# Attentions and moves stand further up in the order, and ScalarE's queue issues the reads of turned blocks

## The chip, the core and the metric

The kernel runs on one core of a Trainium2 chip. Its engines are TensorE (PE, matrix products into PSUM), VectorE (DVE), ScalarE (ACT), GpSimd (POOL) and SyncE (SP), each with an instruction stream of its own that is worked off strictly in order; they wait for each other by semaphores. Sixteen DMA engines move data between HBM and the on-chip SBUF; a DMA is issued by an instruction in some engine's stream. The metric is the device time of one execution, in microseconds (us).

## What is computed

Two transformer blocks of two layers each, on 256 tokens of width 1024, all in float32. A layer of the first block (only the shapes matter here):

```python
h = x @ w_in[l]                                   # 1024 x 9216: q, k, v of three attentions, and gates
o_a = retention(rq, rk, rv, rg)                   # 4 heads, rotary q and k
o_b = chunk_attention(cq, ck, cv, rel_bias)       # 8 heads
o_c = diff_attention(dq, dk, dv)                  # 8 half heads, rotary q and k
merged = g0 * (o_a @ w_branch_a) + g1 * (o_b @ w_branch_b) + g2 * (o_c @ w_branch_c)
x = layer_norm(ALPHA * x + merged @ w_out)
x = layer_norm(ALPHA * x + swiglu(x))
```

A layer of the second block has a swiglu, a mixer (an mLSTM with a short convolution beside a windowed attention aq, ak, av), a second swiglu and a gated embedding.

## The kernel before

**Dense work.** Every product with a weight is cut into "units": 128x1024 floats of weights (two k-tiles of 512 columns), with 12 matmuls for both row tiles, because each product is made from a high and a low part (weights high x input high, low x high, high x low). There are some 780 units. For unit `u` SP loads `raw` (13 buffers, `NR`), ScalarE makes the high part `wh` (10 buffers, `NH`), VectorE the low part `wl`. SP issues the load of unit u+13 and ScalarE the high part of unit u+10 when unit u is done. A chunk of 512 output columns is four units; it is gathered in one of two pairs of PSUM banks, in turn, and its evacuation (`keep`, `gate`, `merge`) has to be over before the next chunk but one starts in the same banks. `keep` is done by ScalarE.

**Side work.** `plan_block1` and `plan_block2` write the steps down once, as one list, and every engine goes through this list and emits its own part of each step. `weave` puts the attention steps (the side) among the dense units; how many units follow each side step is the digit in a table, `UNITS_AMONG_1` for the first block and `UNITS_AMONG_2` for the second. A digit moved is thus a move on all engines at once.

**Moves.** Where rows have to become columns (the rotated rq, rk, dq, dk, the attention outputs rg0, rg1, oc, and ak, aq0, aq1), VectorE transposes 32x32 blocks (`block`), the blocks are written to a scratch in HBM by four DMAs (`out`), read back in turned order by one (`back`), and ScalarE copies (`copy`) or splits (`halve`, with VectorE for the low part) what has landed. The swiglus do the same for every 256 columns (`act_out`, `act_back`, `split_act`), 11 times in each of the six. Before the change SP issues all of these, between the weight loads.

**The stretch of the first block that matters.** In unit order: dq is projected by units 36 to 39, dk by 40 to 43, dv by 44 to 47 (`keep` after each), the gates of branch a by 48 to 55, and `w_branch_a` with the retention's output `oa` is 56 to 63. Unit 48 uses the banks of dk, unit 52 those of dv, and unit 56 waits for `halve` of rg1. POOL rotates dq and dk (`rope`, 12 operations each, in order, semaphore `roped`). The step `load name="bm12"` has SP load the gates' bias into `b_merge`, memory that it shares with the decay and rotation tables; so SP first waits for the last score product of the retention and for the rotation of dk (lines 1217 to 1219); `ln1` right behind it waits for the rotation too.

In the second block `p_split`, `a_square` and `m_log` are small steps of ScalarE ahead of the first convolution chunk (`conv`), whose evacuation by VectorE frees the banks of `mv0`.

Of the kernel before, what the change touches and what calls it, by code (L numbers as in the profile page):

```python
# [15 lines left out]
P = 128  # L16
# [3 lines left out]
KT = D // P  # L20
# [9 lines left out]
NH = 10  # L30


OUT_AT, BACK_AT, LAST_AT = 0, 2, 4


# [2 lines left out]

UNITS_AMONG_1 = "0101110101110001100001010111322201001101000110011010101213311002101010201102232"
UNITS_AMONG_2 = "10000020101100011211002110001101011110011110401001111100100111101101000101020040102"

# [316 lines left out]
def plan_block1(p, t_x):  # L362
# [109 lines left out]
    for j in range(2):  # L472
        merge(1, j, "w_branch_b", "ob", 4, j, ob_o + 1)
    p.weave(before, dense_a + p.begin(), side, UNITS_AMONG_1)

# [157 lines left out]
def plan_block2(p, t_x):  # L633
# [20 lines left out]

    t_x = ffn("ffn1", 0, t_x, after_ffn1)

    def kept_rows(name, c0, dst, off, pair):
        c = p.chunk(("w_in", [(c0, c0 + 512)]), "x", KT, 512, pair, t_x)
        q[name] = p.add("keep_kv" if name == "akv" else "keep", c=c, dst=dst, off=off)

    def convolved(i, pair):
# [6 lines left out]
    for i, (name, c0, dst, off) in enumerate([("akv", 5128, "aqk", 1024), ("aq0", 4104, "aqk", 0),  # L668
                                              ("aq1", 4616, "aqk", 512)]):
        kept_rows(name, c0, dst, off, (i + 1) % 2)  # L670
        if name == "akv":
            p.add("a_ksquare", kept=q["akv"])
        else:
            if name == "aq0":
                p.add("a_knorm")
                p.moved("block", "ak")
            p.moved("block", name, kept=q[name])
    group = p.begin()
    p.steps = before
    p.open(group, OPEN["w_in_2"])  # L680
    p.pair = 0
    c_log = p.chunk(("w_in", [(4096, 4104)]), "x", KT, 8, p.pair, t_x, form="narrow")
    p.add("m_narrow", c=c_log)
    p.add("p_split")
    for r in range(R):
        p.add("a_square", tile=r, kept=(q["aq0"], q["aq1"]), n=p.cc["sumsq"])
# [6 lines left out]
    for i in range(4):  # L693
# [6 lines left out]
        else:  # L700
            c = p.chunk(("w_in", [(3072 + 512 * (i - 2), 3584 + 512 * (i - 2))]), "x", KT, 512, p.flip(), t_x)
# [12 lines left out]
    p.add("m_log", t=p.next_t(), c=c_log)  # L714
    for r in range(R):
        p.add("a_sum", tile=r)
    for what in ("out", "back", "copy"):
        for name in ("ak", "aq0", "aq1"):
            c_a = p.moved(what, name)
    p.add("m_log2")  # L720
    p.add("m_spread", n=p.of_block["aq1"])
    tt, sm = {}, {}
# [24 lines left out]
    c_a = []  # L747
# [8 lines left out]
    for j in range(2):  # L756
        c = p.chunk(("w_branch_m", [(512 * j, 512 * j + 512)]), "hm", KT, 512, p.flip(), t_m)
# [10 lines left out]
    for j in range(2):  # L768
        c = p.chunk(("w_out", [(512 * j, 512 * j + 512)]), "x", KT, 512, p.flip(), t_g)
# [7 lines left out]
    t_x = p.tail(group, lambda tile: rms(p, 2, tile, fed), turned(p, 2, fed), *TAILS["w_out_2"])  # L777
# [15 lines left out]
    for j in range(2):  # L793
# [5 lines left out]
        c = Step("chunk", u=u, pair=1, nth=nth)  # L799
# [13 lines left out]
        else:  # L813
            t_x = p.tail(group, lambda tile: rms(p, 0, tile, fed), turned(p, 0, fed), *TAILS["ple"])
# [95 lines left out]
MOVED = ('rg0', 'rg1', 'oc', 'rq', 'rk', 'dq', 'dk', 'ak', 'aq0', 'aq1')  # L910
# [4 lines left out]
def build(nc, plan, a):  # L915

    with ExitStack() as ctx:
# [71 lines left out]
        act_out = [sem(f"act_out{i}") for i in range(2)]  # L989
        act_back = [sem(f"act_back{i}") for i in range(2)]  # L990
        act_split = sem("act_split")
        blocked = sem("blocked")
        moved_out = {name: sem("out_" + name) for name in MOVED}
        moved_back = {name: sem("back_" + name) for name in MOVED}
# [12 lines left out]
        x, o = mem.at("x", o, [P, R, D])  # L1007
# [6 lines left out]
        b = {}  # L1014
# [27 lines left out]
        c0 = o  # L1042
# [74 lines left out]
        def of2(w, h):  # L1117
# [13 lines left out]
        landed = {**stage,  # L1131
                  "rg0": b["rg"][:, 0, :],
                  "rg1": b["rg"][:, 1, :]}
# [18 lines left out]
        with nc.Block() as block:  # L1152
            @block.sync
            def _(sp):
# [8 lines left out]
                for st in steps:  # L1163
# [13 lines left out]
                    elif st.kind == "out":  # L1177
                        sp.wait_ge(blocked, st.n)
                        to = a["moved"][MOVED.index(st.name)].rearrange("(q j b n) -> b j q n", q=4, j=32, b=4)
                        for k in range(4):  # L1180
                            sp.dma_start(to[k], stage[st.name][32 * k:32 * k + 32, :].rearrange("p (q n) -> p q n", q=4))\  # L1181
                              .then_inc(moved_out[st.name], 16)
                    elif st.kind == "back":
                        sp.wait_ge(moved_out[st.name], 64 * (st.l + 1))
                        sp.dma_start(landed[st.name], a["moved"][MOVED.index(st.name)].rearrange("(p n) -> p n", p=P))\
                          .then_inc(moved_back[st.name], 16)
                    elif st.kind == "act_out":
                        sp.wait_ge(act_turned, st.n)
                        to = a["turn"][st.i].rearrange("(q j b n) -> b j q n", q=4, j=32, b=4)
                        for k in range(4):  # L1190
                            sp.dma_start(to[k], b["ffn_s"][32 * k:32 * k + 32, st.i % 2, :, :].rearrange("p r n -> p (r n)")
                                         .rearrange("p (q n) -> p q n", q=4)).then_inc(act_out[st.n % 2], 16)
                    elif st.kind == "act_back":
                        sp.wait_ge(act_out[st.n % 2], 64 * ((st.n + 1) // 2))
                        sp.dma_start(b["ffn_a"][:, st.i % 2, :, :].rearrange("p r n -> p (r n)"),
                                     a["turn"][st.i].rearrange("(p n) -> p n", p=P))\
                          .then_inc(act_back[st.n % 2], 16)
                    elif st.kind == "load":
                        k, l = st.name, st.l
                        if k == "bias":  # L1200
# [147 lines left out]
            def _(act):  # L1348
# [7 lines left out]
                for st in steps:  # L1356
                    k = st.kind
# [19 lines left out]
                    elif k == "o_split":  # L1377
                        act.wait_ge(o_ready_0, st.m)
                        act.wait_ge(o_ready, st.o + 1)
                        act.activation(split_of[st.dst][0][:, st.h // 2 - 1:st.h // 2 + 1, :],  # L1380
                                       OB[:, :].rearrange("p (k n) -> p k n", k=2), ACT.Copy).then_inc(t_hi, 1)
                    elif k == "copy":
                        act.wait_ge(moved_back[st.name], 16 * (st.l + 1))
                        act.activation(copy_to[st.name].rearrange("p k (r b n) -> p (k r) b n", r=R, b=4),
# [63 lines left out]
                    elif k == "square":  # L1448
                        r, j = st.tile, st.j
# [20 lines left out]
                    elif k == "conv":  # L1470
                        act.wait_ge(unit_done, st.c.u + 1)
                        act.wait_ge(p_conv, 16 * (st.l + 1))
                        for ct in range(2):
                            c = 2 * st.i + ct
# [19 lines left out]
                    elif k == "a_square":  # L1494
                        r = st.tile
# [860 lines left out]
```

## Time and profile before

| what | value |
| --- | --- |
| median of 3 runs | 2307.84 us (2306.3 to 2308.96) |
| the profiled execution: its own time | 2307.95 us |
| its span in the trace | 2306.2 us |
| TensorE busy | 99% |
| VectorE busy | 66% |
| ScalarE busy | 53% |
| POOL busy | 6% |
| DMA, mean over the span | 209 GB/s |

Busy is time in which an engine executes something; PE's matmuls are pipelined, so 99% busy says that little time lies idle between them, not that each is as short as it can be. An idle time has a releaser: the instruction whose semaphore ended the wait.

### The profile page before, as it was taken

Reading aid. Unit: us, or ns where it says so; the run is one execution under the profiler, and the core shown is the slowest. Engines: PE = TensorE matmul, PEld = TensorE weight load, DVE = VectorE, ACT = ScalarE, POOL = GpSimd, SP = SyncE. Lnnn points to the kernel's source line nnn. Section 1 sums busy time; section 2 is a strip of 40 time slices with the busy share of each in tenths; the row PEclk is TensorE's granted clock in tenths of the full one; section 3 lists DMA queues with packets and bytes.
Section 4 is the critical chain, followed back from the end, with each engine's and each line's share of the span. In section 5 each row is a group of like instructions: output and inputs, shape, how many; then the busy total and the mean of one; then the engine's idle time right before and its main releaser. Section 6 shows DMA issues by size and latency. Waiting matters only on the chain.

```text
span 2306.2 us, 30120 instructions
## 1 busy us (share of the span) xinstructions
PE 2283.7 (99%) x11144; PEld 1906.6 (83%) x11144; DVE 1527.7 (66%) x2411; ACT 1233.8 (53%) x1890; POOL 128.6 (6%) x141
## 2 busy tenths in 40 slices
PE   9999999999999999999999999999999999999999
PEld 8887888888878888888878888888888888888887
DVE  6656786566567866576587765664766587657654
ACT  6555544445555454354467654554554478555543
POOL 3140000004300000000000000000000000000000
PEclk9999999999999999999999999999999999999999
DMA  8556568756475587577564444875677564456772
GB/s 336 199 192 238 190 220 290 228 185 214 156 267 186 172 287 242 180 256 248 189 230 157 157 155 165 265 241 195 219 244 238 178 215 156 150 171 209 233 235 89
DMA packets 179857, 483.08 MB, mean 209 GB/s; under 512 B 20480, under 2 KB 65152, under 8 KB 178688
## 3 DMA queue, kind: packets, MB, share of 16 engines
q1 hardware_dynamic: 179712, 481.16, 61.7%
q8 instruction: 90, 1.47, 0.3%
q14 instruction: 55, 0.45, 0.1%
HBM read 452.24 MB, written 28.84 MB: 209 GB/s over the span
## 4 chain that ended last, share of the span: by engine, by line
PE 92%; DVE 3%; DMA 3%; ACT 1%; SPq 1%; issue 1%; POOL 0%; DVEq 0%; ACTq 0%
PE bank L2104 27%; PE bank L2109 27%; PE bank L2108 27%; PE bank L2151 2%; PE bank L2091 2%; PE bank L2092 2%; PE bank L2093 2%; DMA raw<-in_weights 1%; DVE wl L1593 1%; PE bank L2240 1%; SPq L1181 1%; DMA rg<-moved 1%; DMA moved<-rv 0%; PE bank L2202 0%; PE bank L2225 0%
## 5 line engine op out<-in xcount | busy, mean ns | idle before, releaser
L1363 ACT ACTIVATE wh<-raw 128x1024 fp32r<-128x1024 f32 (+1 forms) x778 | 814.5, 1051 | 768.1 <-PE bank L2109 690.8
L1593 DVE TENSOR_TENSOR wl<-raw,wh 128x1024 fp32r<-128x1024 f32 (+1 forms) x778 | 927.8, 1223 | 282.9 <-ACT wh L1363 279.3
L2104 PE MATMUL bank<-wh,xh 128*128 128x512 f32 (+1 forms) x2102 | 826.8, 393 | 5.0 <-issue 3.9
L2109 PE MATMUL bank<-wh,xl 128*128 128x512 f32 (+1 forms) x2102 | 816.8, 389 | 0.0
L2108 PE MATMUL bank<-wl,xh 128*128 128x512 f32 (+1 forms) x2102 | 815.7, 388 | 0.0
L2104 PEld LDWEIGHTS bank<-wh,xh 128*128 128x128 f32 x2102 | 395.2, 188 | 87.0 <-issue 7.3
L2109 PEld LDWEIGHTS bank<-wh,xl 128*128 128x128 f32 x2102 | 394.9, 188 | 81.0
L2108 PEld LDWEIGHTS bank<-wl,xh 128*128 128x128 f32 x2102 | 395.5, 188 | 76.9
L2104 PE MATMUL bank<-wh,act_h 128*128 128x512 f32 x528 | 206.0, 390 | 0.0
L2109 PE MATMUL bank<-wh,act_l 128*128 128x512 f32 x512 | 199.4, 389 | 0.0
L2108 PE MATMUL bank<-wl,act_h 128*128 128x512 f32 x512 | 199.3, 389 | 0.0
L2104 PEld LDWEIGHTS bank<-wh,act_h 128*128 128x128 f32 x528 | 99.1, 188 | 20.2
L2109 PEld LDWEIGHTS bank<-wh,act_l 128*128 128x128 f32 x512 | 96.1, 188 | 20.0
L2108 PEld LDWEIGHTS bank<-wl,act_h 128*128 128x128 f32 x512 | 96.1, 188 | 19.7
L2091 PE MATMUL bank<-xh,wh 128*128 128x256 f32 x384 | 110.6, 288 | 0.0
L2093 PE MATMUL bank<-xh,wl 128*128 128x256 f32 x384 | 108.6, 283 | 0.0
L2092 PE MATMUL bank<-xl,wh 128*128 128x256 f32 x384 | 108.6, 283 | 0.0
L2030 DVE SCALAR_TENSOR_TENSOR ffn_a<-bank,scr,ffn_s 128x256 f32<-128x256 f32 (+1 forms) x96 | 39.6, 457 | 71.1 <-ACT ffn_s L1559 71.0
L1396 ACT ACTIVATE act_h<-ffn_a 128x512 fp32r<-128x512 f32 x66 | 41.6, 630 | 73.4 <-DMA ffn_a<-turn 73.3
L2091 PEld LDWEIGHTS bank<-xh,wh 128*128 128x128 f32 x384 | 73.5, 191 | 1.4 <-issue 1.0
L2092 PEld LDWEIGHTS bank<-xl,wh 128*128 128x128 f32 x384 | 73.6, 192 | 0.1
L2093 PEld LDWEIGHTS bank<-xh,wl 128*128 128x128 f32 x384 | 73.5, 192 | 0.0
(347 smaller groups left out, 2066.9 us busy)
## 6 DMA issues: line engine op xcount, KB each, us to landing
raw<-in_weights SPq DMA_DIRECT2D x760, 512.0 KB, 4.3
turn<-ffn_s SPq DMA_DIRECT2D x264, 64.0 KB, 2.8
ffn_a<-turn SPq DMA_DIRECT2D x66, 256.0 KB, 4.7
raw<-in_weights SPq DMA_DIRECT2D x16, 384.0 KB, 3.2
ln<-in_ln SPq DMA_DIRECT2D x4, 1024.0 KB, 6.8
moved<-merged SPq DMA_DIRECT2D x32, 128.0 KB, 3.5
merged<-moved SPq DMA_DIRECT2D x8, 512.0 KB, 7.0
bias<-in_bias SPq DMA_DIRECT2D x2, 1024.0 KB, 9.3
```

The source lines that it names most:

```text
L1181: sp.dma_start(to[k], stage[st.name][32 * k:32 * k + 32, :].rearrange("p (q n) -> p q n", q=4))\
L1363: act.activation(wh[:, u % NH, 0:used(u)], raw[:, u % NR, 0:used(u)], ACT.Copy).then_inc(hi_done, 1)
L1396: act.activation(b["act_h"][:, 2 * st.i:2 * st.i + 2, :].rearrange("p k (r b n) -> p (k r) b n", r=R, b=4), act_in(st.i), ACT.Copy).then_i ...
L1593: dve.tensor_tensor(wl[:, u % NR, 0:used(u)], raw[:, u % NR, 0:used(u)], wh[:, u % NH, 0:used(u)].bitcast(F32), ALU.subtract).then_inc(lo_ ...
L2030: ins = dve.scalar_tensor_tensor(dst, up, root[:, r:r + 1], s_in, ALU.mult, ALU.mult)
L2091: pe.matmul(out, w_h, lh[:, kt, :], start=st.first and i == 0, stop=False)
L2092: pe.matmul(out, w_h, ll[:, kt, :], start=False, stop=False)
L2093: last = pe.matmul(out, w_l, lh[:, kt, :], start=False, stop=st.last and i == st.nk - 1)
L2104: pe.matmul(out, h, w_h, start=st.first and i == 0, stop=False)
L2108: pe.matmul(out, h, w_l, start=False, stop=False)
L2109: last = pe.matmul(out, lo, w_h, start=False, stop=ends)
L2151: last = pe.transpose(bank[:, i * P:(i + 1) * P], piece, ident[:, :])
```

## The change

`UNITS_AMONG_1` and `UNITS_AMONG_2` get other digits (the line of one stands here for both); out and back of ak, aq0 and aq1 leave the woven side list and are written among the first chunks of the mixer; and all `back` and `act_back` steps are emitted by ScalarE in place of SP, with the same waits. No computation is added or left out.

```diff
+OUT_EARLY = {1: "ak", 2: "aq0"}
...
-UNITS_AMONG_1 = "0101110101110001100001010111322201001101000110011010101213311002101010201102232"
+UNITS_AMONG_1 = "0101110101110001100001010111012101001101000111011011101213311002101010201102244"
...
+    def out_early(i):
+        if i in OUT_EARLY:
+            p.moved("out", OUT_EARLY[i])
+
     def kept_rows(name, c0, dst, off, pair):
-        c = p.chunk(("w_in", [(c0, c0 + 512)]), "x", KT, 512, pair, t_x)
+        c = p.chunk(("w_in", [(c0, c0 + 512)]), "x", KT, 512, pair, t_x, among=out_early if name == "aq1" else None)
...
+    p.moved("back", "ak")
     group = p.begin()
...
     p.add("m_narrow", c=c_log)
+    p.moved("back", "aq0")
+    p.moved("out", "aq1")
     p.add("p_split")
...
-    for what in ("out", "back", "copy"):
-        for name in ("ak", "aq0", "aq1"):
-            c_a = p.moved(what, name)
+    for name in ("ak", "aq0", "aq1"):
+        if name == "aq1":
+            p.moved("back", name)
+        c_a = p.moved("copy", name)
...
-                    elif st.kind == "back":
-                        sp.wait_ge(moved_out[st.name], 64 * (st.l + 1))
-                        sp.dma_start(landed[st.name], a["moved"][MOVED.index(st.name)].rearrange("(p n) -> p n", p=P))\
-                          .then_inc(moved_back[st.name], 16)
...
-                    elif st.kind == "act_back":
-                        sp.wait_ge(act_out[st.n % 2], 64 * ((st.n + 1) // 2))
...
+                    elif k == "act_back":
+                        act.wait_ge(act_out[st.n % 2], 64 * ((st.n + 1) // 2))
...
+                    elif k == "back":
+                        act.wait_ge(moved_out[st.name], 64 * (st.l + 1))
+                        act.dma_start(landed[st.name], a["moved"][MOVED.index(st.name)].rearrange("(p n) -> p n", p=P))\
+                           .then_inc(moved_back[st.name], 16)
```

**SP in the first block.** These are SP's DMAs of the kernel before, from the read-back of rk to the read-back of rg0. The 24 weight loads are those issued when units 24 to 47 are done; `b_merge` is the load "bm12", `ln` is "ln1", and `rv` is the stage from which rg0 and rg1 go out.

```order
L1185 DMA dv<-moved 128x1024 [waits out_rk]
L1168 DMA raw<-in_weights 128x1024 [waits unit_done] x24
L1219 DMA b_merge<-in_b_merge 128x2048 [waits roped,s_done]
L1222 DMA ln<-in_ln 128x2048 [waits roped]
L1168 DMA raw<-in_weights 128x1024 [waits unit_done]
L1181 DMA moved<-rv 32x4x256 [waits blocked]
L1181 DMA moved<-rv 32x4x256 x3
L1168 DMA raw<-in_weights 128x1024 [waits unit_done]
L1181 DMA moved<-rv 32x4x256 [waits blocked]
L1181 DMA moved<-rv 32x4x256 x3
L1168 DMA raw<-in_weights 128x1024 [waits unit_done]
L1185 DMA rg<-moved 128x1024 [waits out_rg0]
```

And this is the same place in the changed kernel, from the way out of rk on.

```order
L1190 DMA moved<-dv 32x4x256 x3
L1177 DMA raw<-in_weights 128x1024 [waits unit_done] x21
L1219 DMA b_merge<-in_b_merge 128x2048 [waits roped,s_done]
L1222 DMA ln<-in_ln 128x2048 [waits roped]
L1177 DMA raw<-in_weights 128x1024 [waits unit_done]
L1190 DMA moved<-rv 32x4x256 [waits blocked]
L1190 DMA moved<-rv 32x4x256 x3
L1177 DMA raw<-in_weights 128x1024 [waits unit_done]
L1190 DMA moved<-rv 32x4x256 [waits blocked]
L1190 DMA moved<-rv 32x4x256 x3
L1177 DMA raw<-in_weights 128x1024 [waits unit_done] x3
```

The read-backs are gone from between the loads, and `b_merge` with its waits has moved from behind the load that unit 47 releases to behind the one that unit 42 releases: five weight loads that stood ahead of it now stand behind it.

**ScalarE at the same place, before.** `wh` is a weight's high part, and the number of its semaphore is the unit modulo 13: `w_loaded1` is unit 53, `w_loaded4` unit 56, `w_loaded5` unit 57. `junk` and `ret_o` are the evacuation of one retention head, `dk` and `dv` the `keep` of those chunks (two row tiles each). First from the high part of unit 53 on, then the `keep` of dv.

```order
L1363 ACTIVATE wh<-raw 128x1024 [waits unit_done,w_loaded1]
L1401 ACTIVATE dk<-bank 128x512 [waits unit_done]
L1401 ACTIVATE dk<-bank 128x512
L1416 ACTIVATE junk,scr<-bank 128x256 [waits o_ready]
L1416 ACTIVATE junk,scr<-bank 128x256 [waits act_chain]
L1418 ACTIVATE ret_o<-bank 128x2x256 [waits act_chain]
L1363 ACTIVATE wh<-raw 128x1024 [waits unit_done,w_loaded2]
```

```order
L1418 ACTIVATE ret_o<-bank 128x2x256 [waits act_chain]
L1363 ACTIVATE wh<-raw 128x1024 [waits unit_done,w_loaded5]
L1401 ACTIVATE dv<-bank 128x512 [waits unit_done]
L1401 ACTIVATE dv<-bank 128x512
L1363 ACTIVATE wh<-raw 128x1024 [waits unit_done,w_loaded6]
```

Now the changed kernel, from the end of the last retention head to the `keep` of dv.

```order
L1426 ACTIVATE ret_o<-bank 128x2x256 [waits act_chain]
L1363 ACTIVATE wh<-raw 128x1024 [waits unit_done,w_loaded0]
L1363 ACTIVATE wh<-raw 128x1024 [waits unit_done,w_loaded1]
L1409 ACTIVATE dk<-bank 128x512 [waits unit_done]
L1409 ACTIVATE dk<-bank 128x512
L1363 ACTIVATE wh<-raw 128x1024 [waits unit_done,w_loaded2]
L1363 ACTIVATE wh<-raw 128x1024 [waits unit_done,w_loaded3]
L1363 ACTIVATE wh<-raw 128x1024 [waits unit_done,w_loaded4]
L1388 DMA rg<-moved 128x1024 [waits out_rg0]
L1363 ACTIVATE wh<-raw 128x1024 [waits unit_done,w_loaded5]
L1409 ACTIVATE dv<-bank 128x512 [waits unit_done]
L1409 ACTIVATE dv<-bank 128x512
```

All four retention heads now stand ahead of the `keep` of dk (before, none did), and the wait for rg0's way out, with its read, stands between the high parts of units 56 and 57, ahead of the `keep` of dv.

**ScalarE in the second block.** The place is the end of chunk aq1 (`aqk`), the high part behind the narrow unit, `p_split` (`p_h`), and the two squares (`wide`, `sq`). Before:

```order
L1401 ACTIVATE aqk<-bank 128x512
L1363 ACTIVATE wh<-raw 128x1024 [waits unit_done,w_loaded9]
L1464 ACTIVATE p_h<-p_raw 128x512 [waits p_emb]
L1500 ACTIVATE wide<-aqk 128x1024 [waits sumsq,d_done2,d_done0]
L1500 ACTIVATE sq_92<-aqk 128x1024 [waits d_done3,d_done1]
```

And in the changed kernel:

```order
L1409 ACTIVATE aqk<-bank 128x512
L1388 DMA mo<-moved 128x1024 [waits out_ak]
L1363 ACTIVATE wh<-raw 128x1024 [waits unit_done,w_loaded9]
L1388 DMA merged<-moved 128x1024 [waits out_aq0]
L1472 ACTIVATE p_h<-p_raw 128x512 [waits p_emb]
L1508 ACTIVATE wide<-aqk 128x1024 [waits sumsq,d_done2,d_done0]
L1508 ACTIVATE sq_92<-aqk 128x1024 [waits d_done3,d_done1]
```

The reads of ak and aq0 now stand ahead of `p_split`; before, SP issued them some units later.

## Rows read from the trace of the kernel before

**Rows 1.** Page, part 1: busy us (share of the span) and instructions, all engines

```profile
PE 2283.7 (99%) x11144; PEld 1906.6 (83%) x11144; DVE 1527.7 (66%) x2411; ACT 1233.8 (53%) x1890; POOL 128.6 (6%) x141
```

**Rows 2.** Waits of the tensor engine, whole span: us in total, times, longest

```profile
PE bank L2104 <- DVE oa_l L1631: 8.2, 2, 4.4
...
PE bank L2104 <- issue: 3.9, 2, 2.0
...
PE bank L2225 <- ACT aqT L1384: 1.4, 1, 1.4
```

**Rows 3.** Timeline of the tensor engine: start, length, what [idle before it]

```profile
186.17 0.47 PE L2104 MATMUL bank<-wh,oa_h 128*128 128x512 f32 x1 [4.35 <-DVE oa_l L1631]
...
668.54 0.77 PE L2104 MATMUL bank<-wh,oa_h 128*128 128x512 f32 x1 [3.82 <-DVE oa_l L1631]
```

**Rows 4.** Windows around both resumptions; granted clock is the third number from the end

```profile
186.00:191.00 5.00, 4.83 (x14) 3.90 (x15) 4.51 (x5) 2.28 (x3) 0.00 (x0) 0.66 0.88 280
667.00:672.00 5.00, 3.46 (x9) 2.83 (x10) 4.94 (x6) 2.18 (x4) 0.00 (x0) 0.66 1.03 364
```

**Rows 5.** Timeline of the tensor engine: retention's score and value products

```profile
146.46 0.59 PE L2158 MATMUL bank<-qT,kT 128*128 128x256 f32 x2
...
147.11 0.60 PE L2254 MATMUL bank<-rv,Pn 128*128 128x256 f32 x2
...
148.41 0.59 PE L2158 MATMUL bank<-qT,kT 128*128 128x256 f32 x2
```

**Rows 6.** Timeline of POOL (one of VectorE): first and last operations of the rotations

```profile
132.15 1.21 POOL L1324 TENSOR_TENSOR rs<-dq,rope 128x256 f32<-128x256 f32 x1 [68.22 <-ACT dq L1401]
...
143.78 1.61 POOL L1329 TENSOR_TENSOR dq<-rs 128x256 f32<-128x256 f32 x1
...
145.52 0.74 POOL L1324 TENSOR_TENSOR rs<-dk,rope 128x256 f32<-128x256 f32 x1
...
149.74 1.30 DVE L1593 TENSOR_TENSOR wl<-raw,wh 128x1024 fp32r<-128x1024 f32 x1
...
150.04 1.60 POOL L1324 TENSOR_TENSOR rs<-dk,rope 128x256 f32<-128x256 f32 x1
...
155.47 0.73 POOL L1329 TENSOR_TENSOR dk<-rs 128x256 f32<-128x256 f32 x1
...
615.35 1.21 POOL L1324 TENSOR_TENSOR rs<-dq,rope 128x256 f32<-128x256 f32 x1 [71.67 <-ACT dq L1401]
```

**Rows 7.** Timeline of ScalarE: two evacuations, and splits of two successive units

```profile
142.97 1.07 ACT L1401 ACTIVATE dk<-bank 128x512 f32<-128x512 f32 x2
...
161.12 1.07 ACT L1401 ACTIVATE dv<-bank 128x512 f32<-128x512 f32 x2
...
168.31 1.06 ACT L1363 ACTIVATE wh<-raw 128x1024 fp32r<-128x1024 f32 x1 [1.66 <-PE bank L2109]
...
171.03 1.06 ACT L1363 ACTIVATE wh<-raw 128x1024 fp32r<-128x1024 f32 x1 [1.66 <-PE bank L2109]
```

**Rows 8.** Timeline of SP's queue: when transfers are issued

```profile
160.54 0.35 SPq L1219 DMA_DIRECT2D b_merge<-in_b_merge  x1
...
162.81 0.33 SPq L1168 DMA_DIRECT2D raw<-in_weights  x1
...
169.49 0.45 SPq L1168 DMA_DIRECT2D raw<-in_weights  x1
...
172.51 0.65 SPq L1185 DMA_DIRECT2D rg<-moved  x1
```

**Rows 9.** DMA issues: size and us to landing, of 162.81 and of 169.49

```profile
raw<-in_weights SPq DMA_DIRECT2D x1, 512.0 KB, 6.9
...
raw<-in_weights SPq DMA_DIRECT2D x1, 512.0 KB, 5.6
```

**Rows 10.** Timeline of ScalarE and VectorE at the second mLSTM block

```profile
1854.97 0.62 ACT L1464 ACTIVATE p_h<-p_raw 128x512 fp32r<-128x512 f32 x1
...
1856.13 0.67 DVE L1851 TENSOR_TENSOR p_l<-p_raw,p_h 128x512 fp32r<-128x512 f32 x1
```

More of the change, by code:

```diff
@@ L30 @@
 NH = 10
+OUT_EARLY = {1: "ak", 2: "aq0"}
 OUT_AT, BACK_AT, LAST_AT = 0, 2, 4
 WARM = (3, 3)
-UNITS_AMONG_1 = "0101110101110001100001010111322201001101000110011010101213311002101010201102232"
-UNITS_AMONG_2 = "10000020101100011211002110001101011110011110401001111100100111101101000101020040102"
+UNITS_AMONG_1 = "0101110101110001100001010111012101001101000111011011101213311002101010201102244"
+UNITS_AMONG_2 = "100110300011211002110001101011110011110401001111100100111101101000101020040102"
 TAILS = {"branch_c": (4, 1, 2, 3), "w_out_1": (8, 6, 5, 5), "ffn_1": (10, 5, 4, 6), "branch_m": (8, 5, 3, 5),
@@ L1192, in _ @@
                                          .rearrange("p (q n) -> p q n", q=4)).then_inc(act_out[st.n % 2], 16)
-                    elif st.kind == "act_back":
-                        sp.wait_ge(act_out[st.n % 2], 64 * ((st.n + 1) // 2))
-                        sp.dma_start(b["ffn_a"][:, st.i % 2, :, :].rearrange("p r n -> p (r n)"),
-                                     a["turn"][st.i].rearrange("(p n) -> p n", p=P))\
-                          .then_inc(act_back[st.n % 2], 16)
                     elif st.kind == "load":
@@ L1381, in _ @@
                                        OB[:, :].rearrange("p (k n) -> p k n", k=2), ACT.Copy).then_inc(t_hi, 1)
+                    elif k == "act_back":
+                        act.wait_ge(act_out[st.n % 2], 64 * ((st.n + 1) // 2))
+                        act.dma_start(b["ffn_a"][:, st.i % 2, :, :].rearrange("p r n -> p (r n)"),
+                                      a["turn"][st.i].rearrange("(p n) -> p n", p=P)).then_inc(act_back[st.n % 2], 16)
+                    elif k == "back":
+                        act.wait_ge(moved_out[st.name], 64 * (st.l + 1))
+                        act.dma_start(landed[st.name], a["moved"][MOVED.index(st.name)].rearrange("(p n) -> p n", p=P))\
+                           .then_inc(moved_back[st.name], 16)
                     elif k == "copy":
```

## Prediction

> **What bounds the kernel now.** I read the page's busy times first: PE is busy for 2283.7 of 2306.2 us [rows 1], so all that an order of steps can give is in the 22.5 us in which PE is idle, and what it can take has no such bound. Next the list of PE's waits [rows 2]: the largest line, 8.2 us in two pieces, is the first unit of `w_branch_a` waiting for `oa_l`, the low part that VectorE makes of the retention's output when it has come back from the scratch; there is one piece for each layer of the first block. Two pieces of 2.0 us (to "issue") and one of 1.4 us (for `aqT`) belong to the mixer of the second block. No line of the list is about the swiglus' moves, so the 66 reads there have no PE time to give back. Then PE's timeline at the two pieces: idle for 4.35 us before 186.17 and for 3.82 us before 668.54 [rows 3]. After each, the granted clock is 0.66 on average over five microseconds [rows 4], that is the lower of the two levels, 1.2 instead of 2.4 GHz, for some 3.4 us, and PE loses (1 - 0.66) x 5 = 1.7 us more. So this wait is worth 8.17 + 3.4 = 11.6 us in all, and it is what the moved steps of the first block are on.
>
> **The change, part by part.** *The old wait.* The retention's end moves five units up (from behind unit 46 to behind unit 41); a unit takes 2.72 us (171.03 - 168.31, two successive high parts, [rows 7]), so its rows are there 13.6 us earlier, and the wait of 4.35 and 3.82 us for `oa_l` loses its old cause: -8.17 us. It comes back only if the moves themselves are held up.
>
> *What is late next.* SP's load of `b_merge` stands behind unit 42's weight load now, behind unit 47's before, and it waits for the rotation of dk, which needs unit 43. Before, that rotation was over at 155.47 + 0.73 = 156.2 [rows 6], and SP came to the load at 160.54 [rows 8] and did not wait for it. In the changed kernel: the retention's products now stand ahead of dk's last unit. A score product takes 147.11 - 146.46 = 0.65 us and a value product 148.41 - 147.11 = 1.30 us [rows 5]; three of the first and four of the second are added ahead of unit 43's end, 7.15 us. The `keep` of dk, at 142.97 before [rows 7], starts at 150.1, and POOL can start on its first half 0.6 us later, at 150.7. (It is free: the rotation of dq, 132.15 to 145.39, moves by two score and one value product, 2.6 us, and ends at 148.0.) The rotation of dk took 145.52 to 156.2, 10.7 us, and that of dq 13.2 us [rows 6]. The difference is what VectorE does beside it: an operation of 0.74 us takes 1.60 where it meets a weight subtraction (150.04 beside 149.74, [rows 6]), twice in the short rotation. In the changed kernel the weight subtractions of at least four units fall into this stretch, behind VectorE's `ret_fin`; I take 12.5 us, nearer to dq's, so the rotation ends at 163.3 (bounds 161.5 and 164.0). The Trainium skill, "SBUF — State Buffer", section "Who interferes with whom", has a rule for it: a VectorE instruction with two SBUF inputs and a GpSimd instruction that reads SBUF exclude each other for a whole instruction; the trace agrees with 1.60 for 0.74 us, and by the rule alone, with four meetings of 0.9 us on 12 x 0.74, the rotation would take some 12.5 us too.
>
> So SP stands still from about 146.5 to 163.3. Five weight loads (units 56 to 60) were issued in that time before. Now unit 56's is issued behind `b_merge` and `ln`, and unit 57's behind the way out of rg0 as well. The same three transfers in a row are in the trace: `b_merge` issued at 160.54, a weight load issued at 162.81 and landed 6.9 us later, at 169.7: 9.2 us from the first issue to the third landing, with one weight load still under way in front [rows 8, 9]. I take 8.2 us without that one (bounds 7.9 and 9.2). The next weight load of the trace, with a way out between, landed at 169.49 + 5.6 = 175.1, 5.4 us behind it [rows 8, 9]; by the mean rate of the first three (2560 KB in 9.2 us) its 1024 KB would take 3.7. I take 4.5 us from unit 56's landing to unit 57's.
>
> ScalarE takes its stream in order: high part of 56, read of rg0, high part of 57, `keep` of dv. From unit 57's landing, one high part (1.06 us) and one `keep` (1.07 us, [rows 7]) make 2.1. So the banks of dv are free at 163.3 + 8.2 + 4.5 + 2.1 = 178.1. PE wants them for unit 52, at the end of unit 51, which stays where it was, since what moved was ahead of it in both orders: about 170.8 (the high part that it releases starts at 171.03, [rows 7]). PE stands idle for 7.3 us; with all low bounds it is 4.4 (161.5 + 7.9 + 3.7 + 2.1 = 175.2), with all high ones 9.9. Before, the `keep` of dv ended at 162.2 [rows 7], with 8.6 us to spare; that spare is the cover, and SP's standstill uses it up. The second layer has the same distances: from dq's rotation to the point where PE was ready for `oa` it is 49.7 us in the one and 49.4 in the other (181.82 - 132.15 and 664.72 - 615.35, [rows 3, 6]).
>
> Knock-on: ScalarE is then some 15 us behind, dk's way out is the last transfer in the backlog, and the copy of dk, which the first `da_s` (moved up from behind unit 60 to behind unit 57) waits for, comes out within a microsecond of PE. I put 0.7 us on it for each layer (bounds 0 and 3). PE's drop to the lower clock behind an idle stretch stays as it is, 1.7 us each time, and cancels.
>
> *Reads on ScalarE's queue.* The trace has no DMA issued by ScalarE. The nearest row is the same instruction on SP, 0.65 us at 172.51 [rows 8]; 86 of them (66 of the swiglus, 20 others) are at most 56 us in 1072 us in which ScalarE is idle [rows 1]. The cover is the ten units of high parts made ahead, and the four units that an evacuation has. In the swiglus I put nothing on it: PE waits for none of their steps in the trace [rows 2], and where the change takes a wait off SP it gives it to ScalarE, with the same release. On the Trainium skill, "DMA: Bandwidth & Descriptors", section "Queues, rings and completion order": SP and ScalarE own a ring each on every DMA engine, served in turn, so a read of ScalarE's would not stand behind SP's backlog. No run here shows it yet; for the sum it would only shift unit 57's landing by part of one read, within the 3.7 to 5.4 above.
>
> *Second block.* The copies of ak and aq0 come several units earlier, which removes the 1.41 us wait for `aqT` in the second layer (the first has none). Against it, ScalarE waits for aq0's way out ahead of `p_split`. VectorE starts its part of that step at 1856.13, 0.54 us after `p_h` is there (1854.97 + 0.62) [rows 10]; a delay of 0.5 to 1.0 us on ScalarE is nearly covered, and what is left over (0 to 0.5 us, I take 0.25) lengthens the 2.0 us wait of each layer, since VectorE works without a pause from there to the first convolution.
>
> **The sum**, against the profiled execution's own 2307.95 us (0.1 us above the median of the runs): layer one -4.35 + 7.3, layer two -3.82 + 7.3, knock-on +1.4, second block -1.4 + 0.5. That is +6.9, so about 2315 us. With the low bounds it is -0.8 (2307), with the high ones +17 (2325). A measurement of this kernel tells about 0.2%, or 4.6 us, from no change.
>
> **The rivals.**
> - *The moves do what the positions say, and nothing takes the wait's place*: both waits go, with their clock losses, and the one of 1.4 us: 2307.95 - 11.6 - 1.4 = 2295 us. For it speaks that everything up to `block` is 13.6 us earlier. Against it: the `keep` of dv would have to end by 170.8, and so the rotation of dk by 156.0, when dk's `keep` starts at 150.1. It decides this way if SP's load turns out not to hold the weights up, or DMA catches up at twice the rate of the rows. 0.13.
> - *One wait for another of the same size*: the rotation in 10.7 us and the faster landings, 4.4 to 5.5 us for each layer, 2307 to 2310 us. For it speaks that each bound has a row. 0.25.
> - *My forecast*, PE idle 5.5 us or more at unit 52: 2310 to 2322, likeliest 2315. 0.54.
> - *ScalarE as the new bottleneck*: its waits for ways out stack up in the mixers or at the swiglus' start, and evacuations are late there as well; a late one costs its lateness and, above some 3 us, 1.7 us of clock: 2 to 3 us at four places more, 2325 and above. Against it: ScalarE is idle 47% of the time. 0.08.
>
> **The numbers.** Faster 0.13 (the first rival), same 0.26 (the second, and the low end of the forecast), slower 0.61. The range has to hold 8 in 10; it leaves out the first rival and the last, 2304 to 2322 us.
>
> **What the changed profile would show.** SP's `b_merge` load at about 163, with an idle stretch of some 15 us before it; ScalarE waiting for `raw` ahead of the high part of unit 56; no PE wait for `oa_l`; in its place PE idle ahead of unit 52, released by ScalarE's `dv` evacuation, 7 us in each layer, and the lower clock behind it; no wait for `aqT`. I am wrong if unit 52 starts near 170.8 (then the step from SP's standstill to the landing of unit 57 is the one that fails), or if PE's waits have grown in the swiglus.

## Result: 16.5 us slower, and the profile after

The changed kernel takes 2323.52 us (median of 4 runs, 2322.46 to 2325.63) against 2307.07 us before (4 runs, 2304.26 to 2308.96). The ratio is 1.0073, with a 95% interval of 1.0058 to 1.0088: slower. Medians and ratios in this document leave out two executions that took far longer than their kernels' others, one of e3 (3826 us) and one of e11 (8148 us). The profiled execution took 2323.73 us with a span of 2322.0 us, which is 15.8 us more than the one before. The first row of the page (busy us, share, instructions) splits that in two.

```profile
PE 2287.1 (98%) x11144; PEld 1908.7 (82%) x11144; DVE 1528.1 (66%) x2411; ACT 1228.4 (53%) x1890; POOL 129.3 (6%) x141
```

PE is idle for 2322.0 - 2287.1 = 34.9 us, where it was 22.5 before [rows 1]: +12.4 us. And its 11144 matmuls, the same ones, are busy for 3.4 us more; the windows below show that more of them ran at the lower clock. PE's waits (us in total, times, longest) say where the idle part is:

```profile
PE bank L2112 <- ACT dv L1409: 15.9, 2, 8.2
PE bank L2112 <- issue: 7.2, 2, 3.8
PE bank L2159 <- DVE merged L1852: 1.7, 2, 1.3
...
PE bank L2112 <- DVE xl L1667: 1.3, 2, 0.7
PE bank L2159 <- DVE Pn L1760: 0.9, 2, 0.4
PE bank L2181 <- ACT kT L1392: 0.6, 1, 0.6
```

The waits for `oa_l` and for `aqT` of [rows 2] are gone. In their place PE waits 7.7 and 8.2 us for ScalarE's evacuation of `dv`, and the two waits "to issue" in the mixers of the second block have grown from 2.0 to 3.5 and 3.8 us.

**The first block.** POOL's timeline at the first and last step of dk's rotation (start, length, what, idle before):

```profile
151.04 2.40 POOL L1324 TENSOR_TENSOR rs<-dk,rope 128x256 f32<-128x256 f32 x1 [5.30 <-ACT dk L1409]
...
163.63 0.74 POOL L1329 TENSOR_TENSOR dk<-rs 128x256 f32<-128x256 f32 x1
```

SP's wait at this load, from its list of waits (us in total, times, longest), and then SP's timeline from the last weight loads ahead of the standstill on:

```profile
SPq L1218 <- POOL dk L1329: 35.0, 2, 17.5
```

```profile
142.50 4.37 SPq L1177 DMA_DIRECT2D raw<-in_weights  x2
164.46 0.33 SPq L1219 DMA_DIRECT2D b_merge<-in_b_merge  x1
164.83 0.43 SPq L1222 DMA_DIRECT2D ln<-in_ln  x1
165.30 0.43 SPq L1177 DMA_DIRECT2D raw<-in_weights  x1
165.78 2.62 SPq L1190 DMA_DIRECT2D moved<-rv  x4
168.45 0.48 SPq L1177 DMA_DIRECT2D raw<-in_weights  x1
```

ScalarE in the same stretch:

```profile
173.90 1.06 ACT L1363 ACTIVATE wh<-raw 128x1024 fp32r<-128x1024 f32 x1 [18.07 <-DMA raw<-in_weights]
175.32 0.33 ACTq L1388 DMA_DIRECT2D rg<-moved  x1
176.56 1.06 ACT L1363 ACTIVATE wh<-raw 128x1024 fp32r<-128x1024 f32 x1 [1.61 <-DMA raw<-in_weights]
177.53 1.06 ACT L1409 ACTIVATE dv<-bank 128x512 f32<-128x512 f32 x2
```

SP issues nothing from 146.9 to 164.46, 0.1 us behind the end of the rotation at 164.37. ScalarE then stands 18.07 us for the weights of unit 56 (173.90), gets those of unit 57 at 176.56, and only behind these two high parts comes the evacuation that PE has been waiting for since 170.99:

```profile
178.69 0.77 PE L2112 MATMUL bank<-wh,xh 128*128 128x512 f32 x1 [7.70 <-ACT dv L1409]
...
667.39 0.77 PE L2112 MATMUL bank<-wh,xh 128*128 128x512 f32 x1 [8.15 <-ACT dv L1409]
```

The clock behind it, in windows of five microseconds (PE's busy time is the first column with an (x), the granted clock stands third from the end):

```profile
173.00:178.00 5.00, 0.00 (x0) 0.00 (x0) 1.57 (x2) 2.49 (x3) 0.00 (x0) 0.57 1.06 395
178.00:183.00 5.00, 4.31 (x10) 3.47 (x11) 2.10 (x2) 3.13 (x5) 0.00 (x0) 0.50 1.03 419
183.00:188.00 5.00, 5.00 (x21) 4.03 (x20) 4.45 (x4) 3.60 (x4) 0.00 (x0) 0.91 1.06 398
...
667.00:672.00 5.00, 4.61 (x11) 3.67 (x12) 1.80 (x2) 3.27 (x4) 0.00 (x0) 0.50 1.02 413
...
1883.00:1888.00 5.00, 4.63 (x13) 3.69 (x14) 4.86 (x9) 2.98 (x5) 0.00 (x0) 0.66 0.05 22
```

Where [rows 4] had 0.66 over the five microseconds behind each wait, this has 0.50 over the whole of them: PE has its matmuls and runs all of them at 1.2 GHz, 10 or 11 in a window that holds 21 later. The last row is a drop in the second layer's mixer that the kernel before did not have there.

**The second block.** SP issues the way out of aq0 in the second layer's mixer:

```profile
1863.99 1.97 SPq L1190 DMA_DIRECT2D moved<-merged  x4
```

and ScalarE, where [rows 10] had `p_h` at 1854.97:

```profile
1865.63 0.33 ACTq L1388 DMA_DIRECT2D mo<-moved  x1
...
1870.63 0.33 ACTq L1388 DMA_DIRECT2D merged<-moved  x1
1871.01 0.63 ACT L1472 ACTIVATE p_h<-p_raw 128x512 fp32r<-128x512 f32 x1 [2.14 <-DMA moved<-merged]
```

VectorE waits for it, and PE comes out later by the same amount:

```profile
1871.67 0.69 DVE L1859 TENSOR_TENSOR p_l<-p_raw,p_h 128x512 fp32r<-128x512 f32 x1 [1.61 <-ACT p_h L1472]
```

```profile
1883.37 0.47 PE L2112 MATMUL bank<-wh,xh 128*128 128x512 f32 x1 [3.75 <-issue]
```

ScalarE stood 2.14 us at the read of aq0, for its way out to land; VectorE was then late by 1.61 us, and PE's wait is 3.75 us, 1.78 more than before.

### The profile page after: what moved, and what is told of

It reads as the page before. It is cut to its first block, busy times and chain, and to the rows that moved or that the text cites. A ratio compares the mean times of both kernels' runs of the same rounds, so it can differ in the third digit from the quotient of the medians.

```text
span 2322.0 us, 30120 instructions
## 1 busy us (share of the span) xinstructions
PE 2287.1 (98%) x11144; PEld 1908.7 (82%) x11144; DVE 1528.1 (66%) x2411; ACT 1228.4 (53%) x1890; POOL 129.3 (6%) x141
## 4 chain that ended last, share of the span: by engine, by line
PE 90%; DVE 4%; DMA 4%; ACT 1%; issue 1%; SPq 0%; POOL 0%; ACTq 0%; DVEq 0%
PE bank L2112 26%; PE bank L2117 26%; PE bank L2116 26%; DMA raw<-in_weights 2%; PE bank L2159 2%; PE bank L2099 2%; PE bank L2100 2%; PE bank L2101 2%; DVE wl L1601 1%; PE bank L2248 1%; PE bank L2210 0%; ACT wh L1363 0%; PE bank L2233 0%; DMA moved<-merged 0%; PE bank L2181 0%
## 5 line engine op out<-in xcount | busy, mean ns | idle before, releaser
L2112 PE MATMUL bank<-wh,xh 128*128 128x512 f32 (+1 forms) x2102 | 828.8, 394 | 24.9 <-ACT dv L1409 15.9
L1659 DVE TENSOR_TENSOR act_l<-ffn_a,act_h 128x512 fp32r<-128x512 f32 x62 | 42.6, 687 | 66.1 <-ACT act_h L1404 65.9
```

The lines of the kernel that those rows point to most:

```text
L1659: dve.tensor_tensor(lo, whole, h.bitcast(F32), ALU.subtract).then_inc(act_split, 1)
L2112: pe.matmul(out, h, w_h, start=st.first and i == 0, stop=False)
```

## Experiments

Theory S: SP's standstill at the load of `b_merge`, with the weights behind it, makes `dv`'s evacuation late; the mixer's loss is ScalarE's wait at the read of aq0. Rival R: the reads on ScalarE's queue hold ScalarE everywhere, at `dv` too. All ratios are to the kernel before on the same chip; "busy" and "idle" are PE's in the profiled execution. Such an execution can lie a few microseconds off its kernel's median, so the ratio decides and the trace says where. In these runs the kernel before had medians of 2305.2 to 2306.9 us.

| | ratio (95%) | median us | PE busy | PE idle |
|---|---|---|---|---|
| before | 1 | 2307.1 | 2283.7 | 22.5 |
| changed | 1.0073 (1.0058 to 1.0088) | 2323.5 | 2287.1 | 34.9 |
| e1 loads late | 1.0007 (0.9999 to 1.0016) | 2307.3 | 2283.4 | 18.8 |
| e2 reads on SP | 1.0043 (1.0030 to 1.0056) | 2314.5 | 2283.5 | 29.7 |
| e3 old order, reads on ScalarE | 1.0018 (1.0008 to 1.0028) | 2308.7 | 2283.0 | 23.5 |
| e4 old first block | 1.0041 (1.0027 to 1.0055) | 2313.7 | 2289.3 | 25.9 |
| e5 = e1 + e2 | 0.9966 (0.9953 to 0.9978) | 2297.7 | 2277.4 | 16.1 |
| e6 wait without load | 1.0102 (1.0087 to 1.0117) | 2329.6 | 2292.5 | 36.4 |
| e7 mixer reads behind squares | 0.9979 (0.9970 to 0.9988) | 2300.0 | 2281.5 | 16.5 |
| e8 copies earlier | 1.0002 (0.9993 to 1.0011) | 2306.7 | 2283.0 | 21.6 |
| e9 mixer's order alone | 0.9979 (0.9969 to 0.9988) | 2302.0 | 2281.4 | 19.0 |
| e10 loads behind dk | 0.9958 (0.9946 to 0.9970) | 2296.7 | 2279.9 | 17.1 |
| e11 swiglu reads on ScalarE | 0.9967 (0.9954 to 0.9980) | 2299.2 | 2280.1 | 16.4 |

**e1, the two loads late.** On the changed kernel (the table gets the digits for it, so that no unit moves):

```diff
-    p.add("load", name="bm12", s=ret_s3, roped=roped)
-    p.add("load", name="ln1", roped=roped)
     for r in range(R):
         h_a = p.moved("out", f"rg{r}", ...)
...
     for src in ("dq", "dk"):
         c_d = p.moved("out", src, ...)
+    p.add("load", name="bm12", s=ret_s3, roped=roped)
+    p.add("load", name="ln1", roped=roped)
```

> The changed kernel, but in the first block of each layer the loads of b_merge (columns D to 3D) and ln1 stand on SP behind the way out of dk (behind unit 48) instead of behind unit 42; nothing else moves. Theory S (SP's standstill): SP waited 17.5 us in each layer for the rotation of dk at this load, unit 56's and 57's weights came late, ScalarE was late with the evacuation of dv. Without that wait the two PE waits for dv (7.7 and 8.2 us, 15.9 together) go, and with them the two stretches at half clock behind them (2.6 us each): 2323.5 - 15.9 - 5.2 = 2302 us, between 2300 and 2306; SP stands still for less than 3 us at the load. Rival R (the reads now on ScalarE's queue hold ScalarE): dv's evacuation is held by ScalarE's own wait for the way out of rg0 and its issue, which stay: PE still idles 4 us or more ahead of unit 52 in each layer, 2312 us or more.

PE's waits in e1:

```profile
PE bank L2112 <- issue: 6.5, 2, 3.4
PE bank L2181 <- ACT kT L1392: 4.2, 2, 2.2
...
PE bank L2159 <- DVE Pn L1760: 1.2, 1, 1.2
```

Both waits for `dv` are gone, with the reads still on ScalarE: theory S holds for the first block and R falls there. The time is 2307.3 us, above the 2300 to 2306 of S: I had left out that something is late next. It is the copy of dk, `kT`, 2.2 and 2.0 us where the changed kernel had one piece of 0.6 us, and `Pn` behind it. ScalarE's timeline shows why `kT` is late:

```profile
184.43 1.06 ACT L1363 ACTIVATE wh<-raw 128x1024 fp32r<-128x1024 f32 x1 [6.14 <-DMA raw<-in_weights]
```

dk had landed at 184.10, but ScalarE stood 6.14 us for a weight that SP had issued behind `b_merge` and `ln`, and made `kT` behind that, at 188.57. So these two transfers, at their later place, still delay the weights behind them.

**e6, the wait without the load.** e1 says that one of two things matters, the wait or the two transfers ahead of the weights. e6 is e1 with the wait alone at the old place:

```diff
+    p.add("load", name="wait", s=ret_s3, roped=roped)
     for r in range(R):
         h_a = p.moved("out", f"rg{r}", ...)
...
+                        elif k == "wait":
+                            sp.wait_ge(s_done, st.s + 1)
+                            sp.wait_ge(roped, st.roped)
```

> The kernel with the late loads, but SP waits at the old place (behind unit 42) for the same semaphores (the rotation of dk) that the load of b_merge waited for, with no transfer there. Theory S (the wait in front of the weight loads is the cause): PE idles ahead of unit 52 again, by what 8.2 us of landings lose through the missing transfers of b_merge and ln: 4 to 6 us in each layer, 2307.3 + 10 + 3.4 to 5 of clock = 2320 us, between 2314 and 2324. Rival V (the volume and place of these two transfers ahead of the weights is the cause): no wait for dv above 1 us, 2307 us within 3.

```profile
PE bank L2185 <- ACT kT L1396: 11.5, 2, 6.0
...
PE bank L2116 <- ACT dv L1413: 7.3, 2, 3.8
```

No less than the whole loss is back (1.0102; 2329.6 us is above my range), with no byte moved at that place: the standstill is the cause of the loss, and it needs no transfer there. The place of the transfers decides where PE pays. Without them in front, unit 56's high part starts at 168.10 instead of 173.90 and unit 57's at 172.60 instead of 176.56, and `dv` costs 3.8 and 3.5 us. `b_merge` and `ln` then stand ahead of later weights, as in e1 (in the first layer 9 us later): ScalarE stands 7.3 and 5.7 us for one of these and comes to dk only afterwards (in the first layer at 198.93, though it had landed at 194.28), and `kT` costs 6.0 and 5.5 us. Not all of e6's distance to e1 is the standstill's: the two mixer waits are 8.4 us together where e1 has 6.5, at steps in which the two kernels are the same, and why they differ isn't shown.

**e2, all reads on SP again**, in the changed order (the two hunks that move `back` and `act_back` to ScalarE are undone).

> The changed kernel's order with all 86 reads back issued by SP again. Theory S: the first block stays as it is (PE idle 7 to 9 us ahead of unit 52 in each layer), since SP's standstill is untouched; only the mixer of the second block can win, where ScalarE no longer stands at a read of aq0 ahead of p_split: the waits there fall from 3.8 to about 2 us each (-3.5 us) and the new drop of the clock at 1884 us goes (-1.7): 2318 us, between 2315 and 2324. Rival R: the waits for dv go or fall below 3 us each; 2308 us or less.

```profile
PE bank L2113 <- ACT dv L1410: 15.8, 2, 8.1
PE bank L2113 <- issue: 3.9, 2, 2.0
```

The first block is untouched by who issues the reads, 15.8 us for `dv` as in the changed kernel; the mixers are back at 2.0 us each. The time, 2314.5 us, is just below the range that I gave: PE's busy time is 3.6 us below the changed kernel's, more than the one clock drop that I had counted.

**e7, the mixer's reads behind the squares.** e1, with ScalarE still issuing them:

```diff
-    p.moved("back", "ak")
...
-    p.moved("back", "aq0")
     p.moved("out", "aq1")
     p.add("p_split")
     for r in range(R):
         p.add("a_square", tile=r, ...)
+    p.moved("back", "ak")
+    p.moved("back", "aq0")
```

> The kernel with the late loads, reads on ScalarE's queue, but in the mixer ScalarE issues the reads of ak and aq0 behind p_split and the two squares instead of ahead of p_split. If ScalarE's wait for aq0's way out is what holds p_split, the two waits of 3.1 and 3.4 us fall to 2.0 and ak's and aq0's copies still come in time: 2307.3 - 2.5, with a clock stretch less 2303 us, between 2301 and 2306. If the cause is the new place of the ways out on SP (traffic, or weights behind them), the waits stay above 3 us and the time at 2307.

ScalarE in e7 at the place:

```profile
1848.10 0.62 ACT L1472 ACTIVATE p_h<-p_raw 128x512 fp32r<-128x512 f32 x1
...
1849.59 0.36 ACTq L1388 DMA_DIRECT2D merged<-moved  x1
```

`p_h` starts without a wait, the two waits "to issue" are 3.9 us together as before the change, and 0.28% is gained on e1, a little more than I had expected (2300.0 us, with 2301 as the low end). The way out of aq0 is on SP at the same place as in e1, so it is the order in ScalarE's queue that cost. The Trainium skill, "PSUM — Partial Sum Buffer", section "Engine vs sequencer instructions", calls ScalarE's queue strictly first in, first out; the trace agrees, with `p_h` held for 2.14 us behind a read in the changed kernel and not held here, where the read stands behind it.

**e4 and e9, the mixer's order alone.** e4 is the changed kernel with the old `UNITS_AMONG_1`; e9 is e4 with all reads on SP.

> The changed kernel with the old table of the first block: only the mixer's order and the reads' queue are new. Theory S: the first block returns to its two waits for oa_l (8.2 us) with 1.7 us of clock each; the mixer keeps what it has in the changed kernel: +3.3 us of longer waits, +1.7 us for the new drop of the clock, -1.4 us for aqT: 2307 + 3.6 = 2311 us, between 2308 and 2313. Rival R: reads on ScalarE cost in the first block too, 2315 us or more.

> The kernel before with one part of the change alone: the new order of ak, aq0 and aq1 in the second block's mixer; the first block's table is the old one and all reads are SP's. With the reads on ScalarE the same kernel took 1.0041 of before. If that loss was the read of aq0 on ScalarE ahead of p_split, it is gone here and the order alone gives back the wait of 1.4 us for aqT: 0.9994 of before (2305 us), between 0.998 and 1.001. If the mixer's order loses by itself (ways out ahead of weights), 1.002 or more.

PE's waits in e4, then in e9:

```profile
PE bank L2112 <- DVE oa_l L1639: 10.3, 2, 5.2
PE bank L2112 <- issue: 8.3, 2, 5.1
```

```profile
PE bank L2113 <- DVE oa_l L1640: 7.0, 2, 3.6
PE bank L2113 <- issue: 3.9, 2, 2.0
```

The same order is 0.2% faster than before with the reads on SP and 0.4% slower with the reads on ScalarE. Both lie outside what I expected, on opposite sides. Of the 14.8 us between the two profiled spans 6.9 are idle time; 7.9 are PE's busy time (2289.3 against 2281.4), that is the clock. The idle part isn't the mixer's alone: the waits there are 4.4 us longer in e4, and those for `oa_l` in the first block 3.3 us (other waits are a little shorter). So, as far as two executions tell, the reads on ScalarE cost in the first block too, in its old order, which theory S did not have (e3 has the same on a smaller scale). The wait for `aqT` is in neither.

**e3, the old order with the reads on ScalarE.**

> The kernel before in its own order, with all 86 reads back issued by ScalarE. Theory S: an issue takes ScalarE 0.33 us and none of its waits in the old order is long, so nothing changes: 2307 us within 3. Rival R: ScalarE is held at the reads in swiglus and blocks, PE's waits grow by some us at several places: 2312 us or more.

PE's wait, and the first high part behind the read of rg0 in ScalarE's timeline, second layer:

```profile
PE bank L2103 <- DVE oa_l L1630: 9.8, 2, 5.4
```

```profile
654.65 1.06 ACT L1354 ACTIVATE wh<-raw 128x1024 fp32r<-128x1024 f32 x1 [2.83 <-DMA moved<-rv]
```

The time is within my 3 us, but the ratio is 0.18% above 1 and its interval leaves 1 out, so "nothing" was too good: ScalarE stands 2.83 us at the read of rg0, and `oa_l`, which is made of what comes behind, is waited for 9.8 instead of 8.2 us. Whether these 1.6 us and a longer time at the lower clock are all of the 0.18% I did not separate.

**e5, e8, e10, e11: what is left when both causes are gone.** e5 is e1 with all reads on SP. e8 is e5 with the copies of dq and dk one unit earlier. e10 is e5 with the loads of `b_merge` and `ln` behind the reads of dq and dk. e11 is e5 with `act_back` alone on ScalarE. Their edits are two digits of the table, the place of two lines, and one hunk of the change.

> The kernel with the late loads of b_merge and ln1, and in addition all reads back on SP's queue. If the two losses are separate (the standstill in the first block; ScalarE's read of aq0 ahead of p_split in the mixer), the mixer's two waits fall from 3.1 and 3.4 to 2.0 us as they did with the reads on SP before, and one stretch at half clock (1.7 us) can go: 2307.3 - 2.5 - 1.7 = 2303 us, between 2300 and 2306. If the reads on SP's queue stand behind its other waits and cost in the first block what they give in the mixer, it stays at 2307 us or more.

> Late loads, reads on SP, and in the first block the copies of dq and dk one unit earlier (behind units 52 and 53), so that ScalarE makes kT before the high part that it stood behind. The two waits of 2.2 and 2.0 us for kT go: 4 us less than the kernel with late loads and reads on SP alone, 2299 us, between 2296 and 2303. If dk's way back has not landed by then, ScalarE stands at the copy and high parts behind it are late: no gain or a loss.

> Late loads and reads on SP as in the fastest kernel so far, but b_merge and ln1 stand behind the reads back of dq and dk (behind unit 51) instead of ahead of them. The way back of dk then has no b_merge and ln in front of it on the DMA engines: its landing comes about 3 us earlier and the waits of 1.8 and 0.7 us for kT go, with the 0.9 us for Pn behind each: 2297.7 - 2.5 = 2295 us, between 2292 and 2298. If dk's landing hangs on the weight loads in front of it and not on these two, it stays at 2298 within 2.

> The same fastest kernel, but the 66 reads of the swiglus alone are issued by ScalarE (0.33 us each), the 20 others by SP. PE waits for none of the swiglus' moves in any trace so far, so nothing changes: 2298 us within 2.5. If these reads hold ScalarE or come at a worse time for DMA, PE's waits grow in the swiglus and the time is 2302 us or more.

e5 is 5 us under my expectation and below its range. Its interval overlaps that of e7, so beyond the two reads in the mixer no gain from SP's queue is shown. Windows over its whole span show no stretch at the lower clock but at the very end, and PE's busy time is the shortest of all:

```profile
PE 2277.4 (99%) x11144; PEld 1902.8 (83%) x11144; DVE 1532.1 (67%) x2411; ACT 1233.1 (54%) x1890; POOL 128.8 (6%) x141
```

e8 was a miss: 2306.7 us, 9 us more than e5. ScalarE's timeline in e8 shows why an earlier place in the queue gave nothing:

```profile
188.15 1.06 ACT L1393 ACTIVATE kT<-merged 128x1024 f32<-128x1024 f32 x1 [0.55 <-DMA merged<-moved]
```

SP issued that read at 175.79; dk landed 12 us later, behind the two loads and the weights. The copy had waited for its data, not for its turn. Why e8 is slower than e5, and not the same, I did not separate: PE is idle for 5.5 us more, 2.9 of them at `Pn`, and busy for 5.6 us more. e10 then moves the two loads away from in front of it, and the wait for `kT` is gone, but `Pn`, made by VectorE, is late instead:

```profile
PE bank L2160 <- DVE Pn L1761: 4.7, 2, 3.4
```

The delay behind the two loads has moved with them: ScalarE now stands 5.2 us for a weight behind `kT`, where in e5 it stood 4.4 ahead of it. The intervals of e10 and e5 overlap (0.9958 and 0.9966), so the step from e5 to e10 is not shown to gain. e10 has the lowest median of this study: 2296.7 us, 0.42% under the kernel before and 1.1% under the changed one by the two ratios. e11 is as fast as e5: the 66 reads of the swiglus cost nothing on ScalarE, as the prediction had it.

## Why the prediction was right in direction and too small

I said slower with 0.61, by PE idle ahead of unit 52 behind SP's standstill, and that is what happened. The time is 1.5 us above the range and 8.5 above the predicted one. The sum, term by term, against the two profiled executions:

| term | put | measured |
|---|---|---|
| old waits for `oa_l` | -8.2 | -8.2 |
| PE idle ahead of unit 52, two layers | +14.6 | +15.9 |
| knock-on at `da_s` (`kT`, `Pn`) | +1.4 | +1.4 |
| wait for `aqT` | -1.4 | -1.4 |
| mixers, two layers | +0.5 | +3.3 |
| clock (PE's busy time) | 0 | +3.4 |
| `xl`, and waits under 0.4 us each | 0 | +1.4 |
| sum | +6.9 | +15.8 |

- *What is late next*: right, step by step. The rotation took 13.3 us (151.04 to 164.37) where I put 12.5, so the load went out 1.2 us later than 163.3 and a little past my bound of 164.0. Unit 56's weights were there 9.4 us behind the load (put 8.2, bound 9.2), unit 57's 2.7 us behind those (put 4.5, bound 3.7): two errors that nearly cancel, in terms whose bounds were too narrow one by one. PE was ready at 170.99 (put 170.8). 7.70 and 8.15 us for 7.3. e1 and e6 show the cause.
- *"PE's drop to the lower clock behind an idle stretch stays as it is, 1.7 us each time, and cancels"*: this step failed. It took a drop as a fixed price, from two rows behind waits of 4 us. Behind the 7.70 us PE worked for 5.2 us at 1.2 GHz (from 178.69 to the return at some 183.9, since the window from 183 has 0.91) and lost half of that, 2.6 us; behind the 8.15 us it was 4.6 us (from 667.39 to 672.0) and 2.3 lost. Against 1.7 each that is 1.5 us more, and the second layer's mixer got a drop of its own, 1.7 us. Together 3.2 us, where PE's busy time says 3.4. The longer wait that replaced the shorter one did not have the same clock loss.
- *"A delay of 0.5 to 1.0 us on ScalarE is nearly covered"*: this step failed too. ScalarE's delay was 2.14 us, since the way out of aq0 was over only 4.7 us behind its last issue (1870.63 against 1863.99 + 1.97). The cover of 0.54 us was there as I had put it, but it leaves 1.60 of 2.14 us: VectorE was 1.61 us late at `p_l` and works without a pause from there to the first convolution, and PE's waits grew by 1.50 and 1.78 us. e7 removes just this. My sum had half a microsecond for both.
- *Reads on ScalarE's queue*: nothing for the swiglus is right (e11). An issue takes ScalarE 0.33 us, not the 0.65 of the row of SP's that I used. It isn't the issue that costs but the wait in front of it, where something urgent stands behind: `p_split`, and a little in the first block (e3).
- *Of the rivals*, "ScalarE as the new bottleneck" had the mixer's mechanism, at two places instead of four, and nearly its price (3.3 us of waits and one clock loss of 1.7 at the two); I kept it apart as a case of its own with 0.08, when it was a part to add to the likeliest one. That, and the clock, is why the range ended 1.5 us too low. The rival's condition for a clock loss, a lateness "above some 3 us", stood in no row, and the kernel before already has a drop behind a wait of 1.97 us (last section).

The Trainium skill, "DMA: Bandwidth & Descriptors", section "Queues, rings and completion order", was the ground for saying that ScalarE's reads travel apart from SP's backlog. The page of the changed kernel agrees as far as the ring goes: its part on DMA queues (packets, MB, share) has a second one, `q10`, for them:

```profile
q1 hardware_dynamic: 167328, 453.36, 59.3%
q10 hardware_dynamic: 12384, 27.79, 3.3%
```

At one place the runs are in line with the rest too. The read of dk, from issue to landing, in e1 (ScalarE's queue, issued at 177.25) and in e5 (SP's, at 176.24, behind the same loads of `b_merge` and `ln`):

```profile
merged<-moved ACTq DMA_DIRECT2D x1, 512.0 KB, 6.9
```

```profile
merged<-moved SPq DMA_DIRECT2D x1, 512.0 KB, 11.3
```

It is no rule for all reads: those of the swiglus take 5.7 us on ScalarE's queue in the changed kernel and 4.7 on SP's before (medians). Nor did it gain time in any run here: e2 and e5, with one queue, are faster than their twins with two.

## What to carry to other kernels

A load that waits for a semaphore on the queue that also feeds the weights is a gate for everything behind it. Here it cost the tensor engine waits of 7.7 and 8.2 us. Before work is pulled ahead, follow each wait of that queue to the work that releases it and ask whether that work has been pulled ahead too. Moving such a load by a few positions was worth 0.66% here (1.0007 against 1.0073), in a kernel whose tensor engine is 99% busy. When a DMA issue moves to a compute engine, price the wait in front of it against the most urgent instruction behind it; the issue itself took 0.33 us here. A big load at a new place also delays what is issued behind it, as the weights ahead of `kT` in e1 show. And when a stall is added to or taken from the tensor engine, add the clock behind it as a term of its own.

## What the runs showed of the hardware that I had not expected

How long the lower clock lasts differs from one drop to the next. Adding up the granted clock over windows of two microseconds, I find 3.4 us at half clock behind the waits of 4.35 and 3.82 us before, 6.8 us at 5.05 and 5.24 us in e4, and 10.2 us around each of the waits of 7.70 and 8.15 us in the changed kernel. There the lower clock began some 5 us before the wait was over, so that PE, idle, paid for about half of it only. It isn't a function of the wait alone: e2 has 6.8 us at a wait of 7.76 and 10.2 us at one of 8.07, and mixer waits of 1.97 us have a drop in some executions and none in others. The kernel before has one, in the first layer's mixer (the wait of 1.97 us ends at 1203.55), and none behind the same wait in the second:

```profile
1203.00:1208.00 5.00, 4.45 (x13) 3.58 (x14) 4.89 (x8) 3.19 (x5) 0.00 (x0) 0.66 1.00 378
...
1867.00:1872.00 5.00, 4.21 (x19) 3.53 (x20) 4.86 (x9) 3.02 (x5) 0.00 (x0) 1.00 1.01 383
```

Over all kernels PE's busy time for the same 11144 matmuls runs from 2277.4 us in e5, which has no such stretch inside its layers, to 2292.5 us in e6, which has six:

```profile
PE 2292.5 (98%) x11144; PEld 1913.0 (82%) x11144; DVE 1529.7 (66%) x2411; ACT 1230.6 (53%) x1890; POOL 128.9 (6%) x141
```

That is 15 us, more than the 12.4 us of idle time that the change added.
